# Block-attention heads of a two-block transformer kernel: output computed transposed, probabilities scaled ahead

## The reference

```
mq, mk = rotary(mq), rotary(mk)              # the first 32 of 128 dimensions of each head
s = (q @ k.T) * 128 ** -0.5                  # 256 x 256, causal mask
p = softmax(s)
o = p @ v                                    # 256 x 128 for each of 8 heads
merged = sigmoid(g_ret) * (o_ret @ w_ret_up) + sigmoid(g_moba) * (o_moba @ w_moba_up)
```

## The kernel before, in words

| Step | TensorE | ScalarE | VectorE |
|---|---|---|---|
| 2 | 4 transposes of QK into banks 4, 5 (L669), after `qk_fixed` and the previous `head_out` | copies them to QKT | |
| 3 | scores: 2 matmuls, 128 and 256 columns, bank 6 (L689) | waits for the maxima; exponentials PR and row sums RS (L1060, L1061) | SC = scale x scores + mask; negated row maxima NM (L1511 to L1518) |
| 5 | 3 transposes of PR, bank 7 (L697), after `probs` | copies them to PT | |
| 6 | values: 3 matmuls of 128 columns, PT stationary, V moving, bank 4 (L706) | | RI = 1/RS (L1527); OF = values x RI (L1533) |
| 7 | 2 transposes of OF, bank 5 (L714), after `o_rows` | U high (L1073), after `ot_done` | U low (L1550), then `head_out` |

## Time and profile before

### The profile page before, as it was taken

One profiled execution on the slowest core, in us unless ns is written; L12 is line 12 of the kernel. 1 busy time (PEld: TensorE's weight loads), 2 busy tenths in 40 slices (PEclk: granted clock), 3 DMA queues, 4 the chain that ended last, 5 costly groups with the idle time before them and its releaser, 6 DMA issues.

```text
span 2488.5 us, 36014 instructions
## 1 busy us (share of the span) xinstructions
PE 2476.3 (100%) x11895; PEld 2055.3 (83%) x11895; DVE 1498.8 (60%) x1798; ACT 1237.0 (50%) x1655; POOL 235.7 (9%) x277
## 2 busy tenths in 40 slices
PE   8999999999999999999999999999999999999999
PEld 7888888878888888888888888888887788877887
DVE  4445445577656777777777776444457555554564
ACT  5445455555445444444444445454547556555443
POOL 0011224231000000000000000010101000432000
PEclk9999999999999999999999999999999999999999
DMA  7655555566655555555555556654564545444654
GB/s 247 194 185 170 169 174 174 175 213 205 209 187 177 187 186 192 185 187 189 189 185 188 188 189 211 201 185 170 171 210 162 170 164 182 163 157 144 228 185 162
DMA packets 131139, 461.08 MB, mean 185 GB/s; under 512 B 14465, under 2 KB 17793, under 8 KB 130433
## 3 DMA queue, kind: packets, MB, share of 16 engines
q1 hardware_dynamic: 122336, 443.60, 53.6%
q10 hardware_dynamic: 8736, 16.58, 2.0%
HBM read 454.36 MB, written 5.77 MB: 185 GB/s over the span
## 4 chain that ended last, share of the span: by engine, by line
PE 97%; DVE 1%; ACT 1%; DMA 0%; issue 0%; POOL 0%; ACTq 0%; POOLq 0%; DVEq 0%; SPq 0%
PE PS L607 21%; PE PS L609 20%; PE PS L608 20%; PE PS L842 13%; PE PS L844 7%; PE PS L866 3%; PE PS L868 3%; PE PS L867 3%; PE PS L689 1%; PE PS L706 1%; PE PS L669 1%; PE PS L648 1%; DVE WL L1466 1%; ACT WH L991 1%; PE PS L781 0%; PE PS L697 0%
## 5 line engine op out<-in xcount | busy, mean ns | idle before, releaser
L1466 DVE TENSOR_TENSOR WL<-RAW,WH 128x1024 fp32r<-128x1024 f32 x842 | 1054.4, 1255 | 934.7 <-ACT WH L991 929.8
L991 ACT ACTIVATE WH<-RAW 128x1024 fp32r<-128x1024 f32 x842 | 890.5, 1060 | 1139.0 <-PE PS L609 746.3
L607 PE MATMUL PS<-WH,HT 128*128 128x512 f32 (+1 forms) x1816 | 725.4, 399 | 5.6 <-DVE HT L1495 3.6
L609 PE MATMUL PS<-WH,HT 128*128 128x512 f32 (+1 forms) x1816 | 708.8, 390 | 0.0
L608 PE MATMUL PS<-WL,HT 128*128 128x512 f32 (+1 forms) x1816 | 707.1, 389 | 0.0
L842 PE MATMUL PS<-HT,WH 128*128 128x512 f32 x1408 | 498.2, 399 | 0.0
L607 PEld LDWEIGHTS PS<-WH,HT 128*128 128x128 f32 x1816 | 341.8, 188 | 78.8 <-issue 8.9
L609 PEld LDWEIGHTS PS<-WH,HT 128*128 128x128 f32 x1816 | 341.2, 188 | 72.0
L608 PEld LDWEIGHTS PS<-WL,HT 128*128 128x128 f32 x1816 | 342.2, 188 | 66.0
L844 PE MATMUL PS<-HT,WL 128*128 128x256 f32 x1408 | 395.8, 281 | 0.0
L842 PEld LDWEIGHTS PS<-HT,WH 128*128 128x128 f32 x1408 | 264.8, 188 | 65.4
(11 more groups left out here) (259 smaller groups left out, 1938.5 us busy)
## 6 DMA issues: line engine op xcount, KB each, us to landing
RAW<-w_stream SPq DMA_DIRECT2D x842, 512.0 KB, 3.3
X<-x_in SPq DMA_DIRECT2D x4, 512.0 KB, 7.4
MEMR<-mem_in ACTq DMA_DIRECT2D x1, 2048.0 KB, 11.5
X<-x_in ACTq DMA_DIRECT2D x4, 512.0 KB, 4.1
x_scratch<-X ACTq DMA_DIRECT2D x4, 512.0 KB, 5.5
X<-x_scratch ACTq DMA_DIRECT2D x1, 2048.0 KB, 8.3
out<-X ACTq DMA_DIRECT2D x8, 256.0 KB, 3.1
bias_scratch<-BE ACTq DMA_DIRECT2D x12, 128.0 KB, 2.5
```

What stands on the lines that cost most here:

```text
L607: pe.matmul(o, hi, WH[:, slot, kk, 0:cols], start=k == 0, stop=False)
L609: ins = pe.matmul(o, lo, WH[:, slot, kk, 0:cols], start=False, stop=k == nq * GK - 1)
L991: act.activation(WH[:, g.slot(j)], RAW[:, g.slot(j)], ACT.Copy).then_inc(hi_split, 1)
L1466: dve.tensor_tensor(WL[:, s], RAW[:, s], WH[:, s].bitcast(F32), ALU.subtract).then_inc(lo_split, 1)
```

## The change

TensorE computes the head's output already transposed. Step 6 becomes two matmuls with V as the stationary side and PT as the moving one, of 256 and of 128 columns, into bank 4; step 7's transposes are gone. ScalarE and VectorE read the output from bank 4 at step 6. The division by the row sum, which was made on the output rows, is made on the probabilities before they are transposed: VectorE does it at its step 4 (`moba_scale`: reciprocal, then two scalings in place of PR, 128 and 256 columns), and TensorE's step 5 waits for the new semaphore `probs_scaled`. V is copied for each head into VH (two buffers) by GpSimd, between the copies of Q and K and the rotation; GpSimd's loop goes over pairs of heads. The other heads of the kernel keep their way.

```diff
+        VH = sb("VH", [P, 2, T, P], F32, at_u2 + 14 * KB)
@@ GpSimd
-            with pool.Fori(0, 8) as h:
-                ch.enter(h, 7)
+            with pool.Fori(0, 4) as i:
+                ch.enter(i, 2 * 8)
+                for r in range(2):
+                    h = i * 2 + r
+                    hold(qk_tr, At(MOBA0 + r, i, 2).count(1))
+                    link(pool.tensor_copy(QK[:, 0, :, 0:P], MQKV[:, :, ds(h * P, P)]))
+                    link(pool.tensor_copy(QK[:, 1, :, 0:P], MQKV[:, :, ds(h * P + W, P)]))
+                    link(pool.tensor_copy(VH[:, r], MQKV[:, :, ds(h * P + 2 * W, P)]))
@@ TensorE
+            def moba_probs(H, M):
+                pe.wait_ge(probs_scaled, M.count(1))
+                head_probs(MOBA, H)
+
+            def moba_output(H, r):
+                pe.wait_ge(pt_ready, H.count(1))
+                pe.matmul(PS[:, 4, 0:S], VH[:, r, 0], PT[:, 0:S], start=True, stop=False)
+                ins = pe.matmul(PS[:, 4, P:S], VH[:, r, 1], PT[:, S:CAUS], start=False, stop=True)
+                ins.then_inc(ot_done, 1)
+                pe.sem_inc(pv_done, 1)
@@
-                    h = i * 2 + r
-                    st = head_steps(MOBA, At(MOBA0 + r, i, 2), lambda s: MQKV[:, s, ds(h * P + 2 * W, P)], (2, 3, 5, 6, 7))
-                    if p - 8 * r in st:
-                        st[p - 8 * r]()
+                    H = At(MOBA0 + r, i, 2)
+                    if p - 8 * r == 2:
+                        head_transpose(MOBA, H, 2)
+                    elif p - 8 * r == 3:
+                        head_scores(MOBA, H)
+                    elif p - 8 * r == 5:
+                        moba_probs(H, At(r, i, 2))
+                    elif p - 8 * r == 6:
+                        moba_output(H, r)
@@ ScalarE
-                    st = head_steps(MOBA, At(MOBA0 + r, i, 2), At(r, i, 2), i * 2 + r, None, (2, 3, 5, 7))
+                    st = head_steps(MOBA, At(MOBA0 + r, i, 2), At(r, i, 2), i * 2 + r, None, (2, 3, 5, 6))
@@ VectorE
+            def moba_scale(H):
+                dve.wait_ge(probs, H.count(1))
+                link(dve.reciprocal(RI[:], RS[:]))
+                dve.tensor_scalar(PR[:, 0:P], PR[:, 0:P], RI[:, 0:1], None, ALU.mult)
+                dve.tensor_scalar(PR[:, P:CAUS], PR[:, P:CAUS], RI[:, 1:2], None, ALU.mult).then_inc(probs_scaled, 1)
+                dve.sem_inc(o_rows, 1)
@@
-                        st = head_steps(MOBA, At(MOBA0 + r, i, 2), At(r, i, 2), i * 2 + r, None, (3, 6, 7))
-                        if p - 8 * r in st:
-                            st[p - 8 * r]()
+                        H = At(MOBA0 + r, i, 2)
+                        if p - 8 * r == 3:
+                            head_scores(MOBA, H, At(r, i, 2), i * 2 + r)
+                        elif p - 8 * r == 4:
+                            moba_scale(H)
+                        elif p - 8 * r == 6:
+                            head_output(MOBA, H, i * 2 + r)
```

More of the change, by code:

```diff
@@ L327, in build @@
         probs = sem("probs")
+        probs_scaled = sem("probs_scaled")
         pt_done = sem("pt_done")
@@ L464, in _ @@
             hold(prod_free, 2 + 6)
-            with pool.Fori(0, 8) as h:
-                ch.enter(h, 7)
[L467 to L474, removed]
+            with pool.Fori(0, 4) as i:
[6 more added lines that the diff above has]
+                    link(pool.tensor_copy(VH[:, r], MQKV[:, :, ds(h * P + 2 * W, P)]))
+                    v = JK[:, 0:128].rearrange("p (z a t d) -> p z a t d", z=2, a=2, t=T)
+                    tab = [con(n).rearrange("p (a t d) -> p a t d", a=2, t=T) for n in ("mcos", "msin")]
+                    rotate(QK[:, :, :, 0:16], QK[:, :, :, 16:32], tab[0], tab[1], v[:, 0], v[:, 1], qk_fixed)
+            ch.leave(4)
             hold(prod_free, 2 + 6 + 4)
@@ L1070, in head_output @@
                 nd = br["dv"] // P
+                bank = 4 if br is MOBA else 5
                 for c in range(nd):
                     dst = U[br["u"]][:, ds(h * nd + c, 1), 0, :]
-                    ins = act.activation(dst, PS[:, 5:6, c * S:(c + 1) * S], ACT.Copy,
+                    ins = act.activation(dst, PS[:, bank:bank + 1, c * S:(c + 1) * S], ACT.Copy,
                                          scale=par("ret", h * nd + c) if br is RET else 1.0)
@@ L1544, in head_output @@
                     hi, lo = u[:, ds(h * nd + c, 1), 0, :].bitcast(F32), u[:, ds(h * nd + c, 1), 1, :]
-                    ps = PS[:, 5:6, c * S:(c + 1) * S]
+                    ps = PS[:, bank:bank + 1, c * S:(c + 1) * S]
                     if br is RET:
```

## The result

The changed kernel takes 2501.44 us (median of 6, 2499.17 to 2503.03) against 2490.56 for the kernel before: a ratio of 1.0043, interval 1.0031 to 1.0054. It is 0.43% slower; 2502.2 had been forecast. The profiled execution took 2503.03, its span 2501.2.

What follows compares the result with a forecast made beforehand. TensorE, running its program in order, was taken to bound the kernel. Stalls of 14.3 us plus 0.6 for the V copy less 3.5 saved gave +11.4 us, so 2502.2 us, range 2499.5 to 2507.

Steps and rivals of the forecast that it cites:

- the wait at step 5: TensorE, before the transposes of PR: waits for VectorE's scaled probabilities in all eight heads, 14.3 us in sum.
- The size of the stall: TensorE before the transposes of PR: 1.57 us in the first head, 1.72 in each of the next six.
- The V copy: GpSimd, ahead of the first head's rotation: paid once, 0.6 us; hidden in the other seven heads.
- The ready time: VectorE's step 4: scaled tile ready 1.95 us after the split's start, the pair of scalings taking 0.61.
- Head 7: Last head's stall before the transposes of PR: 2.4 us taken, 2.7 if GpSimd's 1.50 us operation blocks the scalings.
- The clock: TensorE's clock falls after each stall: +13.6 us, 2516, chance 0.04; after the last head's alone 2504, chance 0.1.
- What TensorE saves: Output transposes of step 7 gone, 3.3 us; cheaper value matmuls at step 6, 0.2 us; together 3.5 us.
- The sum: Whole kernel: stalls 14.3 plus GpSimd's copy 0.6 less TensorE's savings 3.5, +11.4 us.
- Rival (a): Step 5: scaling ready in time, only the gain left, 2487.9 us; chance 0.07 within 0.2%, 0.02 faster.
- Rival (c): GpSimd and VectorE block each other in every head: 0.3 to 1 us a head, 2504 to 2508, chance 0.07.
- The other signs: Profile after: TensorE idles 1.4 to 1.6 us (last 2.2), first head's step 2 wait 1.0, step 6 0.65, busy down some 3.

Runs made afterwards that it cites:

- pool_held: The changed kernel with GpSimd's start on the first retention head held until the eighth head's probabilities are scaled: 2498.96 us.

## Why the prediction was right, point by point

- **What bounds the kernel, and the wait at step 5.** Right: eight waits put down to the scaling, at the place and for the reason named. The run with the scaling alone and the run without it show how the cost divides.
- **The size of the stall.** 1.57 for head 0 was 1.51. 1.72 for heads 1 to 6 was 1.51 too: I took VectorE's lateness in these heads from a trace where a rotation step of GpSimd was in flight as the split of step 3 began, and made it 1.38 long. The V copy moved GpSimd's chain out of that spot: with it alone the split of step 4 is 0.15 us earlier against step 5, and in the run with the scaling alone, which has no V copy, these heads have 1.43 idle and not 1.30. An edit can remove a collision as well as make one; I had looked only for the second.
- **The ready time.** 1.95 us from the start of the split to the scaled tile was 1.89 (169.76 - 167.87); the scalings take 0.29 and 0.35, overlapped.
- **Head 7.** I took 2.4 of 2.0 to 2.7. From start to start it is 346.42 to 349.78 in the second profile, 3.36 - 0.79 = 2.6, nearly the blocked case. The late split of step 4 was in the forecast; of the block I had all on the scalings, and it fell half on that split (0.24) and half on the first scaling (0.27). The Trainium skill ("SBUF — State Buffer", section "SBUF: two separate sides") gives the port pair that VectorE and GpSimd share as an exclusive lock. The trace agrees: the scaling begins at 348.36 beside an operation of GpSimd that ends at 348.84, and is over at 348.92, after 0.56 us; it takes 0.29 with GpSimd held back.
- **The clock.** This was a term of the range and should have been one of the sum. I gave a fall behind head 7 alone a chance of 0.1; both profiles of the changed kernel have it, though two of its eleven executions can't have had it (the mean clock, above). By the forecast's own words, "a granted clock below 1" would show it wrong, and in head 7 that came true: the mechanism was right for the stalls and wrong on this point. The stall of 2.2 by the matmul ends, between a harmless row of 1.25 and a harmful one of 3.58, was not "near the harmless one".
- **What TensorE saves.** Forecast 3.5. The run without the scaling gives 3.3, with a V copy of 0.5 in it: 3.8. The output costs 0.66 (173.83 - 172.72 - 0.454, head 0), forecast 0.65.
- **The V copy.** 0.6 forecast, 0.50 on the trace, 0.4 by the medians. Hidden in heads 1 to 7, as said.
- **The sum.** 7 x 1.51 + 2.6 + 1.7 + 0.5 - 3.8 = +11.6, against 10.9 of the medians: stalls 1.3 too large in heads 1 to 6, a clock of 1.7 too few. That the forecast of 11.4 lies so close is in part luck: these two go against each other.
- **Rival (a)**, the scaling in time, decided "once the split of step 4 begins before about 164.5". True to the letter, but I hadn't looked at the other way to meet it: the scaling in front of the split, into the 2.0 us of idle time in the earlier trace rows. It gives 2486.8, where I had worked out 2487.9 for the case: 3.3 below its kernel before, and not 2.9.
- **Rival (c)**, blocks in every head, isn't seen: in heads 1 to 6 the idle time is the 1.30 of head 0. An operation of GpSimd does lie beside the split of step 3 there, but it is GpSimd's operation that takes longer (1.30 and not 0.32, at 189.12 in head 1), while the split takes its 1.23.
- **The other signs.** The idle times were 1.30 and not 1.4 to 1.6 (2.30 in the last, 2.2 forecast), head 0's step 2 waited 0.87 and not 1.0, step 6 cost 0.66. TensorE's busy time isn't down by 3 us, because of the clock; without a stall it is.

## What to carry to other kernels

When an operation is moved from a free place to one on which the engine that bounds the kernel waits, what counts is when it will be done, and not how long it takes: here 0.6 us of VectorE work in each head cost 14 us in all, and nothing when it stood one instruction earlier in VectorE's program. Look at what stands in front of it there, and above all at an idle time before that. Where a new idle time of TensorE is unavoidable, keep it well below the lengths at which the traces show its clock falling: behind head 7's stall of 2.6 us the fall cost 1.6 to 1.7 more.

## What the hardware showed beyond expectation

Idle times of TensorE of 1.30 to 1.44 us never let its clock fall: 7 in each of two profiles of the changed kernel, 8 in pool_held, 7 in the scaling alone, 29 in all. Those of 2.09 us did in 4 of 7, those of 2.88 in 4 of 7, those of 2.29 to 2.30 in 3 of 3 profiles, and 4.09 and 5.46 each time they occurred. Above some length, then, equal stalls have unequal prices, here none or 5 to 12 matmuls at 1.2 GHz (1.0 to 2.4 us). The idle time of 3.5 to 3.8 us ahead of the product at 19.4 us, which all twelve profiles have, lost 1.7 us by the granted clock in ten profiles and 3.4 in two. The Trainium skill ("TensorE: Matmul & The Clock Gate", "Part 1: The HAM clock gate") has an idle stretch put the engine back to its throttled default; these runs agree, and add that shorter ones than 3.58 us do it, sometimes.
